# Three-layer fp32 block: the last feed-forward norm by products with ones, and two weight sums per layer by transfers that add

## The chip, the cores and the metric

One NeuronCore of one Trainium2 chip runs the whole program. The metric is device time in microseconds (us), median of several runs. The engines are TensorE (PE, with its weight loads as PEld), VectorE (DVE), ScalarE (ACT), GpSimd (POOL) and SyncE (SP). [...]

## The reference, cut to what matters

Two blocks follow each other over 512 tokens of width 1024, in fp32: three attention layers in all, and behind each of them a gated feed-forward layer (FFN) with a hidden width of 2816. All else (gated linear attention, band, memory, differential and forgetting attention) stays as it is in the change.

```
x = x + conv_ffn(rmsnorm(x, norm_ffn_g[l]), ...)          # layers 0 and 1
h2 = rmsnorm_2(x, norm2_g[l])                             # layer 2, eps 1e-5
g = jnp.einsum('bsd,df->bsf', h2, w_gate[l])
u = jnp.einsum('bsd,df->bsf', h2, w_up[l])
x = x + jnp.einsum('bsf,fd->bsd', jax.nn.silu(g) * u, w_down[l])
```

In layers 0 and 1 g also goes through a causal convolution of three taps before the silu.

## The kernel before, in words

**Layout.** Activations lie transposed: 1024 features as 8 tiles `X[:, k, :]` of 128 partitions by 512 tokens. Each fp32 operand is split into a high and a low fp32r part (`hH`, `hL` for activations, `WH`, `WL` for weights), and every product is done three times: high by high, low by high, high by low. SP loads weights into six places of `raw`; ACT copies a piece into `WH` (rounding it) and DVE subtracts to get `WL` (steps `conv` for whole units of 128x2048, `cconv` for pieces of 128x1024, "chunks").

**Norms.** The scale of a token, 1/sqrt(mean square), isn't applied to the input but to the products, through `Rsb` (128x512, one row per token repeated over partitions). The squares are added over the 8 tiles into `acc`: tiles 1 to 6 on POOL (`res_norm`, L3264), tile 7 on DVE (`res_last`, L3005). Then there are two ways to sum over the partitions:

- the norms in `ROW_NORMS` ("ffn0", "kv", "ffn1"): ACT and DVE split `acc` into `accH` and `accL` (`row_split`), PE multiplies both by a matrix of ones (two products of 128x512, `row_sums`), so the sums come out on all partitions; ACT takes the root into `Rsb`, DVE inverts all 128x512 of it (`row_inverse`, L2742);
- the norm "n2" of layer 2: PE multiplies four pieces of `acc` by a column of ones (`rstd_first`, L1379), ACT takes the root of 128x4, DVE inverts 128x4, PE spreads that over the partitions with four products by the identity (`rstd_second`, L1391), and ACT copies the result into `Rsb`. These products are in plain fp32.

**The FFN.** The first one or two of 11 steps (`WHOLE` = 2, 2, 1 for layers 0, 1, 2) are done plainly: units of gate and up weights, `whole` or `half` tiles (L1497, L1516). All later steps split the products into blocks A11, A12, A21, A22 by features and gate or up and do seven products in place of eight (`PRODUCTS` = 1, 5, 6, 3, 7, 2, 4; L1846, 24 matmuls of 128x256 each), with sums of inputs (`wtB`, `wtS`, `wtL` make them in `Tf`, `TH`, `TL`) and sums of weights: product 5 needs A21+A22, product 6 adds A11 to that, 3 adds A12 to that of 6, and 7 needs A11+A21. A sum of weights is one DVE addition of 128x1024 (`wsum`, L2547) into `Wsum[0]` (5, 3) or `Wsum[1]` (6, 7), then split by `cconv` like any piece. Products 1, 6, 7 and 4 gather in one PSUM bank and ACT copies it out between them (`wcopy`, L2063): 6 waits for the copy of 1, 3 waits for that of 5, 7 for that of 6, 4 for that of 7.

**Order.** A planner, `order()`, writes one list of steps; each engine walks through it and does its part of each step, in that order, with semaphores between the engines. In the attention output (`out_rest`) eight tiles m = 0..7 come out of PE; for each, DVE adds to `X`, ACT makes `hH` and the square, DVE `hL`, and POOL adds the square to `acc`. In `ffn_wino` the order around the first products is written out by hand; in layer 2 `sum_ahead` puts the first two `wsum` steps between the `wtS` and `wtL` steps, in layers 0 and 1 `conv_ahead` puts them in front of the `cconv` steps. POOL issues the transfers that add the FFN's partial outputs to `X` (`wx`, L3288), DMA with an accumulating write.

Of the kernel before, what the change touches and what calls it, by code (L numbers as in the profile page):

```python
# [34 lines left out]
WHOLE = (2, 2, 1)  # L35
# [8 lines left out]
BLOCKS = {1: ("A11",), 5: ("A21", "A22"), 6: ("A11",), 3: ("A12",), 7: ("A11", "A21"), 2: ("A12",), 4: ("A22",)}  # L44
SUMS = (5, 6, 3, 7)


# [118 lines left out]
def chunk_list():  # L166

    chunks, items, seen = [], [], set()
    for n, u in enumerate(UNITS):
        role = u[6] if len(u) > 6 else None  # L170
        if role is None or role[1] == "T":
            items.append(("unit", n))
            continue
        i = role[0]
        if i in seen:
            continue
        seen.add(i)
        for key in dict.fromkeys(SEQUENCE[i]):
            c = {"key": (i,) + key, "i": i, "sum": None, "unit": None}
            if key[0] == "q":  # L180
                _, s, q = key
                parts = [ROLE[i, b, s] for b in BLOCKS[q]]
                if q in SUMS:
                    c["sum"] = {6: [(i, "q", s, 5)], 3: [(i, "q", s, 6)]}.get(q, []) + parts
                    c["place"] = {5: 0, 6: 1, 3: 0, 7: 1}[q]
                else:
                    c["unit"] = parts[0]
            else:
                c["unit"] = ROLE[(i, "D") + key[1:]]
            items.append(("chunk", len(chunks)))  # L190
            chunks.append(c)
    return chunks, items
# [26 lines left out]
def raw_read_last():  # L219

    out = {}
    for at, (kind, x) in enumerate(ITEMS):
        if kind == "unit":
            out[x] = at, ("wl", x, last_part(x))
            continue
        c = CHUNKS[x]
        for n, when, key in ([(c["unit"], at, ("wl", "c", x))] if c["unit"] is not None else
                             [(y, at - 1.5, ("wg", "sum", x)) for y in c["sum"] if not isinstance(y, tuple)]):
            out[n] = max(out.get(n, (-1, None)), (when, key), key=lambda v: v[0])
    return out  # L230
# [90 lines left out]
def pieces(hd):  # L321
# [3 lines left out]
    if hd % 2 == 0:  # L325
# [11 lines left out]
             "C": ([4, 5, 0, 1, 2, 3, 6, 7], 6)}  # L337
ROW_NORMS = ("ffn0", "kv", "ffn1")
NEXT_NORM = {"A": "ffn0", "B": "ffn1", "C": "n2"}
# [8 lines left out]
def order():  # L348
# [8 lines left out]
    def conv_ahead(end):  # L357
        while now["conv"] < len(ITEMS):
# [204 lines left out]
    def out_rest(stage, nrm):  # L563
# [3 lines left out]
        while opened:  # L567
# [6 lines left out]
            if m:  # L574
                for x in (0, 1) if m == 1 else (m,):
                    tile_done("res_norm", stage, x, nrm)
            m += 1
        for u in range(2, 4):
            n = take()
            for c in (0, 128):  # L580
# [4 lines left out]
                for x in T_SUMS.get(m, ()):  # L585
                    put(x[0], WINO_OF[nrm], x[1])
                m += 1

    def ffn_wino(i, end):
# [16 lines left out]

        def sum_ahead(i):
            c = now["summed"]
            while CHUNKS[c]["i"] < i or not CHUNKS[c]["sum"]:
                c += 1  # L610
            put("wsum", c)
            now["summed"] = c + 1

        def whole(name, m, n):
# [402 lines left out]
def program(nc, wall, xt, memt, colsd, biasd, consts, rope, gatew, out):  # L1017
    ctx = ExitStack()
    with ctx:
# [168 lines left out]
        s_raw = [sem(f"raw{i}") for i in range(6)]  # L1188
        s_part = [sem(f"part{i}") for i in range(2)]
        s_mem = [sem(f"mem{i}") for i in range(4)]  # L1190
        s_x = [sem(f"x{i}") for i in range(8)]
# [113 lines left out]
        def chunk_slot(c):  # L1305
            x = W_AT["chunk", c]
            o = (x % 2) * CHUNK
            return [v[x // 2][:, o:o + CHUNK] for v in (WH, WL)]

        def chunk_src(c):  # L1310
# [648 lines left out]
        def scalar(e):  # L1959
            w, mark = Lane(e), partial(ev.mark, "act")  # L1960

            for what, *a in STEPS:
                if what == "start":
                    src = memt.rearrange("p (k t) -> p k t", k=8)
                    for i in range(4):
                        e.dma_start(mrA[:, 2 * i:2 * i + 2, :], src[:, 2 * i:2 * i + 2, :]).then_inc(s_mem[i], 16)
                    w.wait_ge(*at("eps", 1))
                    e.activation(small[:, 62:63], small[:, 60:61], ACT.Copy).then_inc(*mark("wh", "warm"))
# [20 lines left out]
                elif what == "cconv":  # L1989
                    c = a[0]  # L1990
                    if CHUNKS[c]["sum"]:
                        w.wait_ge(*at("wg", "sum", c))
                    else:
# [137 lines left out]
                elif what == "rstd_first":  # L2131
                    w.wait_ge(*at("sums", a[0]))
                    w.wait_ge(*at("eps", 1))
                    eps = a[1]
# [335 lines left out]
        def vector(e):  # L2470
# [44 lines left out]
            for what, *a in STEPS:  # L2515
# [18 lines left out]
                elif what == "wsum":  # L2534
                    c = CHUNKS[a[0]]
                    src = []
                    for y in c["sum"]:
                        if isinstance(y, tuple):
                            w.wait_ge(*at("wg", "sum", CHUNK_AT[y]))
                            src.append(Wsum[CHUNKS[CHUNK_AT[y]]["place"]][:, :])  # L2540
# [648 lines left out]
        def gpsimd(e):  # L3189
            w, mark = Lane(e), partial(ev.mark, "pool")  # L3190

            for what, *a in STEPS:
                if what == "start":
                    e.memset(diag[:, :], 0.0).then_inc(*mark("set", "zero"))
                    e.memset(gw[:, :, :], 0.0).then_inc(*mark("set", "gw0"))
                    e.memset(small[:, 60:61], 1e-6).then_inc(*mark("eps", 0))
                    e.memset(small[:, 63:64], 1e-11).then_inc(*mark("eps", 2))
                    e.memset(small[:, 61:62], 1e-5).then_inc(*mark("eps", 1))
                    for n, (c, size) in enumerate(V_ONES):
                        e.memset(vA[:, :, c:c + size], 1.0).then_inc(*(mark("set", "vones") if n else mark("set", "vonesh")))  # L3200
                    w.wait_ge(s_K if ev.sems else None, 16)
                    for i, j in ((0, 0), (1, 2), (2, 3)):
                        e.tensor_copy(KB[:, i, :], K[:, j, :]).then_inc(*mark("KB", i))

# [124 lines left out]
        def sync(e):  # L3329
# [34 lines left out]
            for h, k, n in STORES:  # L3364
# [19 lines left out]
        RCOL_USED = {"mix0": [], "kv": [("vev", "vA", 2, 2)], "n1": [("vev", "vB", 2, 2)],  # L3384
                     "n2": [("vev", "fv", 2, 1)], "last": [("spread", "n2")]}

# [129 lines left out]
```

## Time and profile before

| | |
|---|---|
| median of 3 runs | 1771.16 us (1771.16 to 1771.86) |
| profiled execution: its own time, its span | 1771.75 us, 1770.0 us |
| busy, share of the span: PE, PEld, DVE, ACT, POOL | 99%, 86%, 73%, 54%, 12% |
| mean granted TensorE clock | 0.998 of full speed |
| weights and other bytes moved by DMA | 205.19 MB, 116 GB/s on the mean |
| FFN of layer 0, 1, 2 begins (first L1497 product) | 260.54, 827.76, 1413.86 us |

The span runs from the first to the last instruction; the run's own time is 1.75 us longer. A timeline row gives the start, the duration (of all of a merged row's instructions together), engine, line, operation, operands, count, and in brackets the engine's idle time before it with what ended that. PE's rows overlap, since its matmuls are pipelined: what a product costs PE is the distance from its start to the next start, not its duration.

### The profile page before, as it was taken

How to read it: one execution, taken by the hardware profiler on the slowest of the kernel's cores; microseconds unless marked ns; L12 is line 12 of the kernel's file. 1: busy time of each engine (PE TensorE's matmuls, PEld its weight loads, DVE VectorE, ACT ScalarE, POOL GpSimd, SP SyncE). 2: the span in 40 equal slices, each digit the busy share in tenths (PEclk: the TensorE clock that was granted, in tenths of full speed). 3: DMA queues.
4: the chain of work that ended last, by engine and by line, in shares of the span. 5: the costliest groups of instructions: out<-in, count | busy, mean ns of one | idle time of the engine just before them, and what ended most of it. 6: DMA issues, size and time to landing. Idle time of an engine off the chain costs nothing.

```text
span 1770.0 us, 26240 instructions
## 1 busy us (share of the span) xinstructions
PE 1759.2 (99%) x10680; PEld 1527.0 (86%) x10680; DVE 1295.2 (73%) x1794; ACT 950.3 (54%) x1442; POOL 203.7 (12%) x223
## 2 busy tenths in 40 slices
PE   9999999999999999999999999999999999999998
PEld 7877788999999887787899999977777899999997
DVE  6878568888786765646888787689767487776765
ACT  6645444655555544755465555552567455454454
POOL 0001220110111200002011110103001101111110
PEclk9999999999999999999999999999999999999999
DMA  6221223654545342212364554443221236555442
GB/s 250 72 90 66 71 95 108 155 138 137 143 127 136 89 158 99 96 49 93 98 178 113 154 127 140 111 119 107 73 96 50 103 99 151 135 143 143 109 141 73
DMA packets 61623, 205.19 MB, mean 116 GB/s; under 512 B 7344, under 2 KB 9520, under 8 KB 53184
## 3 DMA queue, kind: packets, MB, share of 16 engines
q1 hardware_dynamic: 38832, 162.55, 27.6%
q0 software_dynamic: 17280, 31.46, 10.0%
q10 hardware_dynamic: 5392, 9.51, 1.7%
q8 instruction: 85, 1.39, 0.3%
q14 instruction: 34, 0.28, 0.0%
HBM read 169.38 MB, written 2.13 MB: 97 GB/s over the span
## 4 chain that ended last, share of the span: by engine, by line
PE 89%; DVE 6%; ACT 3%; issue 1%; DMA 1%; ACTq 0%; DVEq 0%; POOL 0%; SPq 0%
PE ps L1846 31%; PE ps L1497 17%; PE ps L1872 16%; PE ps L1411 6%; PE ps L1536 4%; PE ps L1659 2%; PE ps L1704 2%; PE ps L1556 2%; PE ps L1684 2%; PE ps L1895 2%; DVE WL L2531 1%; PE ps L1743 1%; PE ps L1724 1%; PE ps L1913 1%; ACT WH L1986 1%
## 5 line engine op out<-in xcount | busy, mean ns | idle before, releaser
L1846 PE MATMUL ps<-hH,WH 128*128 128x256 f32 x896 | 253.9, 283 | 0.8 <-ACT held L2063 0.8
L1846 PE MATMUL ps<-hH,WL 128*128 128x256 f32 x896 | 254.0, 283 | 0.0
L1846 PE MATMUL ps<-hL,WH 128*128 128x256 f32 x896 | 253.9, 283 | 0.0
L2553 DVE TENSOR_TENSOR WL<-raw,WH 128x1024 fp32r<-128x1024 f32 x138 | 168.2, 1220 | 113.1 <-ACT WH L1997 113.1
L2531 DVE TENSOR_TENSOR WL<-raw,WH 128x1024 fp32r<-128x1024 f32 (+1 forms) x137 | 167.5, 1260 | 89.3 <-ACT WH L1986 88.9
L1497 PE MATMUL ps<-hH,WH 128*128 128x512 f32 x528 | 208.7, 395 | 0.3 <-DVE WL L2531 0.3
L1497 PE MATMUL ps<-hH,WL 128*128 128x512 f32 x528 | 205.9, 390 | 0.0
L1497 PE MATMUL ps<-hL,WH 128*128 128x512 f32 x528 | 205.9, 390 | 0.0
L3288 POOL DMA_DIRECT2D X<-sq x120 | 104.8, 959 | 866.3 <-ACT sq L2052 864.4
L1846 PE MATMUL ps<-TH,WL 128*128 128x256 f32 x672 | 190.5, 283 | 0.0
L1846 PE MATMUL ps<-TL,WH 128*128 128x256 f32 x672 | 190.4, 283 | 0.0
L1846 PE MATMUL ps<-TH,WH 128*128 128x256 f32 x672 | 190.4, 283 | 0.0
L2553 DVE TENSOR_TENSOR WL<-Wsum,WH 128x1024 fp32r<-128x1024 f32 x112 | 136.7, 1221 | 68.4 <-ACT WH L1997 68.2
L1986 ACT ACTIVATE WH<-raw 128x1024 fp32r<-128x1024 f32 (+1 forms) x137 | 134.5, 1028 | 78.8 <-PE ps L1497 39.6
L1846 PEld LDWEIGHTS ps<-hH,WH 128*128 128x128 f32 x896 | 172.1, 192 | 2.1 <-ACT held L2063 1.0
L1846 PEld LDWEIGHTS ps<-hL,WH 128*128 128x128 f32 x896 | 172.2, 192 | 1.2
L1846 PEld LDWEIGHTS ps<-hH,WL 128*128 128x128 f32 x896 | 172.1, 192 | 0.0
L1872 PE MATMUL ps<-FH,WH 128*128 128x512 f32 x432 | 168.9, 391 | 0.0
L1872 PE MATMUL ps<-FL,WH 128*128 128x512 f32 x432 | 168.9, 391 | 0.0
L1872 PE MATMUL ps<-FH,WL 128*128 128x512 f32 x432 | 168.3, 389 | 0.0
L1997 ACT ACTIVATE WH<-raw 128x1024 fp32r<-128x1024 f32 x138 | 144.5, 1053 | 19.5 <-PE ps L1846 16.8
L1997 ACT ACTIVATE WH<-Wsum 128x1024 fp32r<-128x1024 f32 x112 | 118.0, 1054 | 55.6 <-PE ps L1846 42.4
(442 smaller groups left out, 3897.7 us busy)
## 6 DMA issues: line engine op xcount, KB each, us to landing
raw<-in_wall SPq DMA_DIRECT2D x166, 512.0 KB, 4.3
raw<-in_wall SPq DMA_DIRECT2D x65, 1024.0 KB, 4.8
X<-sq POOLq DMA_DIRECT2D x120, 256.0 KB, 4.0
bias<-in_bias ACTq DMA_DIRECT2D x12, 256.0 KB, 3.0
raw<-in_wall SPq DMA_DIRECT2D x8, 256.0 KB, 7.0
X<-in_xt SPq DMA_DIRECT2D x8, 256.0 KB, 7.8
CB<-rows ACTq DMA_DIRECT2D x8, 256.0 KB, 3.4
out_y<-X SPq DMA_DIRECT2D x8, 256.0 KB, 2.2
```

The lines of the kernel that those rows point to most:

```text
L1411: mm = e.matmul(ps[b][:, :], ww[:, k, c:c + 128], x, start=(k == seq[0] and i == 0), stop=(k == seq[-1] and i == 2))
L1497: mm = e.matmul(ps[b][:, 0:N], ww[:, k, c:c + 128], x[:, k, 0:N], start=(k == 0 and i == 0), stop=(k == 7 and i == 2))
L1536: mm = e.matmul(o, x[:, k, t * 128:t * 128 + 128], ww[:, k, :], start=(k == 0 and i == 0), stop=(k == 7 and i == 2))
L1556: mm = e.matmul(ps[b][:, :], x[:, k, t * 128:t * 128 + 128], ww[:, kx, :], start=(k == 0 and i == 0), stop=(k == 7 and i == 2))
L1659: mm = e.matmul(ps[b][:, c:c + L], queries[u["kind"]][r, u["m"], t * 128:t * 128 + 128], keys[u["kind"]][r, u["m"], 0:L], start=opens, sto ...
L1846: mm = e.matmul(ps[b][:, 256 * u:256 * u + 256], ww[:, p, 128 * u:128 * u + 128], x, start=(opens and p == 0 and u == 0 and n == 0), stop= ...
L1872: mm = e.matmul(ps[BANK["wd", i, g, m]][:, :], ww[:, kx, mi * 128:mi * 128 + 128], x[:, f % 8, :], start=(kx == 0 and n == 0), stop=(kx == ...
L1986: e.activation(WH[W_AT["unit", n] // 2][:, c], unit_raw(n)[:, c], ACT.Copy).then_inc(*mark("wh", n, x))
L1997: e.activation(chunk_slot(c)[0], chunk_src(c), ACT.Copy).then_inc(*mark("wh", "c", c))
L2531: e.tensor_tensor(WL[v][:, c], unit_raw(n)[:, c], WH[v][:, c].bitcast(F32), ALU.subtract).then_inc(*mark("wl", n, x))
L2553: e.tensor_tensor(L, chunk_src(c), H.bitcast(F32), ALU.subtract).then_inc(*mark("wl", "c", c))
L3288: e.dma_start(X[:, m, :], part[m % 2][:, :], accum_op=ALU.add).then_inc(s_part[m % 2], 16)
```

## The change

The norm "n2" joins `ROW_NORMS`, so that layer 2 goes the way of layers 0 and 1 (its epsilon stays in column 61), and the other branch of `ffn_wino` goes. For the first seven-product step of each layer the sums for products 5 and 6 are no longer made by DVE: POOL issues, among the last steps of the attention output, two plain transfers of 512 KB from the weights in memory into `Wsum[0]` and `Wsum[1]` (behind tile m = 1), one accumulating transfer into each (behind m = 3) and a third into `Wsum[1]` (behind m = 5), five for each layer. A transfer that adds waits on POOL until the one before it into the same place has landed. The blocks themselves are still loaded into `raw` for the other products. `sum_ahead` goes; ACT's `cconv` of these two pieces and DVE's sum for product 3 wait for the transfers' semaphores. Two groups of POOL's semaphore marks become part of another one, with the same waits.

```
+DMA_SUMS = {5: ("A21", "A22"), 6: ("A11", "A21", "A22")}
+DMA_ROUNDS = (((0, 5, 0), (1, 6, 0)), ((0, 5, 1), (1, 6, 1)), ((1, 6, 2),))
+DMA_AT = {1: 0, 3: 1, 5: 2}
...
+                c["dma"] = s == WHOLE[i] and q in DMA_SUMS
...
-ROW_NORMS = ("ffn0", "kv", "ffn1")
+ROW_NORMS = ("ffn0", "kv", "ffn1", "n2")
...
-                        if CHUNKS[c]["sum"]:
+                        if CHUNKS[c]["sum"] and not CHUNKS[c]["dma"]:
                             put("wsum", c)
...
+            if m in DMA_AT:
+                put("wdma", WINO_OF[nrm], DMA_AT[m])
...
-        if st in ROW_NORMS:
-            put("row_split", st)
+        put("row_split", st)
         n = take()
-        if st in ROW_NORMS:
-            put("sqrt_table", st)
+        put("sqrt_table", st)
         whole("g", 0, n)
-        if st in ROW_NORMS:
-            put("wtS", i, 1)
-            half(1, n, 0)
-            put("row_sums", st, 60)
-            put("wtL", i, 1)
-            half(1, n, 1)
-            put("row_inverse", st)
-            put("wtB", i, 2)
-            put("wtS", i, 2)
-        else:
-            put("rstd_first", st, 61)
-            put("wtS", i, 1)
-            put("wtL", i, 1)
-            put("wtB", i, 2)
-            put("wtS", i, 2)
-            whole("g", 1, n)
-            put("rstd_second", st)
+        put("wtS", i, 1)
+        half(1, n, 0)
+        put("row_sums", st, 61 if i == 2 else 60)
+        put("wtL", i, 1)
+        half(1, n, 1)
+        put("row_inverse", st)
+        put("wtB", i, 2)
+        put("wtS", i, 2)
         done.add(n)
-        if WHOLE[i] == 1:
-            sum_ahead(i)
         put("wtL", i, 2)
         put("wtB", i, 3)
         if WHOLE[i] == 1:
             put("wtS", i, 3)
-            sum_ahead(i)
             put("wtL", i, 3)
...
                 elif what == "cconv":
                     c = a[0]
                     if CHUNKS[c]["sum"]:
-                        w.wait_ge(*at("wg", "sum", c))
+                        w.wait_ge(*summed(c))
...
+                elif what == "wdma":
+                    i, r = a
+                    w.wait_ge(*at("out", OUT_OF[i], 0))
+                    for x, pn, n in DMA_ROUNDS[r]:
+                        if n:
+                            w.wait_ge(s_wsum[x] if ev.sems else None, 16 * (len(DMA_SUMS[pn]) * i + n))
+                        y = ROLE[i, DMA_SUMS[pn][n], WHOLE[i]]
+                        src = wall[:, WOFF[y]:WOFF[y + 1]]
+                        if n:
+                            e.dma_start(Wsum[x][:, :], src, accum_op=ALU.add).then_inc(s_wsum[x], 16)
+                        else:
+                            e.dma_start(Wsum[x][:, :], src).then_inc(s_wsum[x], 16)
```

## Rows read from the trace of the kernel before

**Rows 1.** The page: busy time, share of the span and instructions of each engine.

```profile
PE 1759.2 (99%) x10680; PEld 1527.0 (86%) x10680; DVE 1295.2 (73%) x1794; ACT 950.3 (54%) x1442; POOL 203.7 (12%) x223
```

**Rows 2.** PE's waits in the whole span: total, times, longest, in us.

```profile
PE ps L1421 <- POOL diag L3194: 1.4, 1, 1.4
...
PE ps L1846 <- ACT held L2063: 0.8, 1, 0.8
```

**Rows 3.** Timeline of PE in layer 2, start of the FFN to the third of the seven products.

```profile
1413.86 0.39 PE L1497 MATMUL ps<-hH,WH 128*128 128x512 f32 x1
...
1426.50 0.48 PE L1497 MATMUL ps<-hH,WH 128*128 128x512 f32 x1
...
1437.47 0.28 PE L1846 MATMUL ps<-hH,WH 128*128 128x256 f32 x1
...
1443.23 0.28 PE L1846 MATMUL ps<-TH,WH 128*128 128x256 f32 x1
```

**Rows 4.** Timeline of PE in layer 0, first gate tile and first up tile.

```profile
260.54 0.39 PE L1497 MATMUL ps<-hH,WH 128*128 128x512 f32 x1
...
271.88 0.39 PE L1497 MATMUL ps<-hH,WH 128*128 128x512 f32 x1
```

**Rows 5.** Timeline of PE in layer 1, products 1, 5 and 3 of the first seven-product step.

```profile
879.92 0.28 PE L1846 MATMUL ps<-hH,WL 128*128 128x256 f32 x1
880.18 0.35 PE L1846 MATMUL ps<-TH,WH 128*128 128x256 f32 x1
...
886.91 0.39 PE L1846 MATMUL ps<-hH,WH 128*128 128x256 f32 x1 [0.77 <-ACT held L2063]
```

**Rows 6.** Timeline of DVE in layer 0, from the last square to the third low part.

```profile
263.36 0.67 DVE L3005 TENSOR_TENSOR acc<-acc,sq 128x512 f32<-128x512 f32 x1
...
271.54 3.35 DVE L2742 RECIPROCAL Rsb<-Rsb 128x512 f32<-128x512 f32 x1
...
277.42 0.96 DVE L2583 TENSOR_TENSOR TL<-Tf,TH 128x768 fp32r<-128x768 f32 x1 [0.92 <-ACT TH L2010]
```

**Rows 7.** Timeline of DVE in layer 2, from the last square to the sum for product 3.

```profile
1417.56 0.68 DVE L3005 TENSOR_TENSOR acc<-acc,sq 128x512 f32<-128x512 f32 x1
...
1426.08 1.22 DVE L2547 TENSOR_TENSOR Wsum<-raw,raw 128x1024 f32<-128x1024 f32 x1
1427.21 0.95 DVE L2583 TENSOR_TENSOR TL<-Tf,TH 128x768 fp32r<-128x768 f32 x1
...
1431.92 1.21 DVE L2553 TENSOR_TENSOR WL<-raw,WH 128x1024 fp32r<-128x1024 f32 x1
...
1435.39 1.21 DVE L2547 TENSOR_TENSOR Wsum<-Wsum,raw 128x1024 f32<-128x1024 f32 x1
```

**Rows 8.** Timeline of ACT in layer 2, from the last high part to the copy of product 1.

```profile
1430.03 0.85 ACT L2010 ACTIVATE TH<-Tf 128x768 fp32r<-128x768 f32 x1 [2.11 <-DVE Tf L2576]
...
1437.76 2.01 ACT L1997 ACTIVATE WH<-Wsum 128x1024 fp32r<-128x1024 f32 x2 [4.97 <-PE ps L1497]
...
1442.13 0.58 ACT L2063 ACTIVATE held<-ps 128x512 f32<-128x512 f32 x1
```

**Rows 9.** Timelines of DVE and ACT in layer 1: second sum, copy of product 5.

```profile
877.68 1.22 DVE L2547 TENSOR_TENSOR Wsum<-Wsum,raw 128x1024 f32<-128x1024 f32 x1
...
886.28 0.58 ACT L2063 ACTIVATE held<-ps 128x512 f32<-128x512 f32 x1
```

**Rows 10.** Timeline of POOL in layer 2: adds of squares 3 and 4, and of square 6.

```profile
1403.20 3.25 POOL L3264 TENSOR_TENSOR acc<-acc,sq 128x512 f32<-128x512 f32 x2 [4.17 <-ACT sq L2338]
...
1415.37 1.72 POOL L3264 TENSOR_TENSOR acc<-acc,sq 128x512 f32<-128x512 f32 x1 [4.33 <-ACT sq L2338]
```

**Rows 11.** Accumulating transfers by source line (ns, landing in us), and issues of weight loads.

```profile
L3288 POOL DMA_DIRECT2D X<-sq x120: 850/862/1236, 311.8 to 1739.2; - x120
...
DMA to landing us min/median/max: 3.2/4.0/9.1
...
raw<-in_wall SPq DMA_DIRECT2D x166, 512.0 KB, 4.3
```

More of the change, by code:

```diff
@@ L178, in chunk_list @@
         for key in dict.fromkeys(SEQUENCE[i]):
-            c = {"key": (i,) + key, "i": i, "sum": None, "unit": None}
+            c = {"key": (i,) + key, "i": i, "sum": None, "unit": None, "dma": False}
             if key[0] == "q":
@@ L227, in raw_read_last @@
         for n, when, key in ([(c["unit"], at, ("wl", "c", x))] if c["unit"] is not None else
-                             [(y, at - 1.5, ("wg", "sum", x)) for y in c["sum"] if not isinstance(y, tuple)]):
+                             [(y, at - 1.5, ("wg", "sum", x)) for y in c["sum"]
+                              if not c["dma"] and not isinstance(y, tuple)]):
             out[n] = max(out.get(n, (-1, None)), (when, key), key=lambda v: v[0])
@@ L586, in out_rest @@
                     put(x[0], WINO_OF[nrm], x[1])
+                if m in DMA_AT:
+                    put("wdma", WINO_OF[nrm], DMA_AT[m])
                 m += 1
@@ L605, in ffn_wino @@
         st = FFN_NORMS[i]
[L607 to L612, printed above, removed]
         def whole(name, m, n):
@@ L1189, in program @@
         s_part = [sem(f"part{i}") for i in range(2)]
+        s_wsum = [sem(f"wsum{i}") for i in range(2)]
         s_mem = [sem(f"mem{i}") for i in range(4)]
@@ L1308, in chunk_slot, with summed @@
             return [v[x // 2][:, o:o + CHUNK] for v in (WH, WL)]
+        def summed(c):
+            c = CHUNKS[c]
+            if c["dma"]:
+                x = c["place"]
+                return (s_wsum[x] if ev.sems else None), 16 * len(DMA_SUMS[c["key"][3]]) * (c["i"] + 1)
+            return at("wg", "sum", CHUNK_AT[c["key"]])
         def chunk_src(c):
@@ L1966, in scalar @@
                         e.dma_start(mrA[:, 2 * i:2 * i + 2, :], src[:, 2 * i:2 * i + 2, :]).then_inc(s_mem[i], 16)
-                    w.wait_ge(*at("eps", 1))
+                    w.wait_ge(*at("set", "eps1"))
                     e.activation(small[:, 62:63], small[:, 60:61], ACT.Copy).then_inc(*mark("wh", "warm"))
@@ L2132, in scalar @@
                     w.wait_ge(*at("sums", a[0]))
-                    w.wait_ge(*at("eps", 1))
+                    w.wait_ge(*at("set", "eps1"))
                     eps = a[1]
@@ L2538, in vector @@
                         if isinstance(y, tuple):
-                            w.wait_ge(*at("wg", "sum", CHUNK_AT[y]))
+                            w.wait_ge(*summed(CHUNK_AT[y]))
                             src.append(Wsum[CHUNKS[CHUNK_AT[y]]["place"]][:, :])
@@ L3195, in gpsimd @@
                     e.memset(gw[:, :, :], 0.0).then_inc(*mark("set", "gw0"))
-                    e.memset(small[:, 60:61], 1e-6).then_inc(*mark("eps", 0))
-                    e.memset(small[:, 63:64], 1e-11).then_inc(*mark("eps", 2))
-                    e.memset(small[:, 61:62], 1e-5).then_inc(*mark("eps", 1))
+                    e.memset(small[:, 60:61], 1e-6).then_inc(*mark("set", "eps0"))
+                    e.memset(small[:, 63:64], 1e-11).then_inc(*mark("set", "eps2"))
+                    e.memset(small[:, 61:62], 1e-5).then_inc(*mark("set", "eps1"))
                     for n, (c, size) in enumerate(V_ONES):
@@ L3202, in gpsimd @@
                     for i, j in ((0, 0), (1, 2), (2, 3)):
-                        e.tensor_copy(KB[:, i, :], K[:, j, :]).then_inc(*mark("KB", i))
+                        e.tensor_copy(KB[:, i, :], K[:, j, :]).then_inc(*mark("set", "KB", i))
                 elif what == "fence":
@@ L3384, in program @@
         RCOL_USED = {"mix0": [], "kv": [("vev", "vA", 2, 2)], "n1": [("vev", "vB", 2, 2)],
-                     "n2": [("vev", "fv", 2, 1)], "last": [("spread", "n2")]}
+                     "last": [("vev", "fv", 2, 1)]}
         SQ_USED = {("ffn0", 1): [("cvD", "k", 5, 3)], ("ffn0", 2): [("cvD", "k", 4, 3)],
```

## The prediction, made before the change was run

> **What bounds the kernel now.** I read the page first: PE is busy 99% of the span, DVE 73% [rows 1]. That share overstates PE, so I looked at the distance between starts, which is what a product costs. In layer 2 the 48 products of 128x512 from 1426.50 to 1437.47 take 0.229 us each, the 48 of 128x256 from there to 1443.23 take 0.12 us each [rows 3]: PE goes at one pace without a hole. Then I read the view of waits, for PE alone: nine entries in the whole span, from 1.4 us at the start to 0.2 us, and only one of them in the part that the change touches, 0.8 us before a seven-product step (L1846) [rows 2]. So work taken from DVE is worth time only where PE waits for it, and work that is added to DVE or POOL costs time only where it makes PE wait. Two numbers decide: what PE itself no longer does, and which product is late next.
>
> **PE's own work, layer 2.** From the first gate product to the first up product layer 2 takes 1426.50 - 1413.86 = 12.64 us [rows 3], layer 0, which already goes the new way, 271.88 - 260.54 = 11.34 us [rows 4], for the same 48 products. The next 48 take 10.97 us [rows 3], 0.09 over the 10.88 of 48 starts at layer 0's pace (11.34 us less two sum products, 50 products in all: 0.227 each). PE is thus done with its plain products 1.30 + 0.09 = 1.39 us earlier. Product 1 could start at 1437.47 - 1.39 = 1436.08 and product 6 at 1443.23 - 1.39 = 1441.84, if their weights and copies are there.
>
> **What DVE and ACT gain and lose in layer 2.** Added: ACT's high and DVE's low part of `acc`, a full 128x512 inversion of 3.35 us (in layer 0's row [rows 6]). Removed: two sums of 1.22 us [rows 7]. These sums stood where DVE would otherwise wait for ACT: in layer 0, without them, the low part at 277.42 had 0.92 us of waiting ahead of it [rows 6], in layer 2 the one at 1427.21 had none behind the sum at 1426.08 [rows 7]. So much of the removed work was free. I follow the new chain with intervals between rows:
>
> - DVE's last square of layer 2 stays at 1417.56 [rows 7].
> - In layer 0 the inversion begins 271.54 - 263.36 = 8.18 us behind that square, and the low part of the third input sum 277.42 - 271.54 = 5.88 us behind the inversion [rows 6]. In layer 2 that gives 1425.74 and 1431.62; the latter stood at 1427.21 before, so it is 4.4 us later.
> - From there to ACT's high part of the last input sum: 1430.03 - 1427.21 = 2.82 us [rows 7, 8], so 1434.44.
> - From that to DVE's low part of product 1's weights: 1431.92 - 1430.03 = 1.89 us [rows 7, 8], so 1436.33, done 1.21 us later at 1437.54. Product 1 can't start at 1436.08; it starts at about 1437.65, 0.2 us later than before. PE's whole gain is eaten here.
> - From product 1's low part to the sum for product 3 (two low parts and two scalings of gate tiles lie between): 1435.39 - 1431.92 = 3.47 us [rows 7], so 1439.80 to 1441.01.
> - ACT walks its list in order. It copies product 3's weights only behind that sum, and behind that copy stand a table load, two silus and the copy of product 1 out of PSUM. Before, the sum was long done and ACT waited for PE (4.97 us); the pair of weight copies ended at 1437.76 + 2.01 = 1439.77, and product 1's copy began 2.36 us later, at 1442.13 [rows 8]. Now: 1441.04 + 1.00 (half the pair) + 2.36 = 1444.40, done 0.58 us later at 1444.98.
> - Product 6 goes on in the bank of product 1, so it waits for that copy: about 1445.03 against 1443.23 [rows 3]. **Layer 2: +1.8 us.**
>
> Behind it product 3 needs product 5's copy, about three ACT operations later; ACT is now 2.27 us behind its old place and PE 1.8 us, so 0.5 us of whatever slack was there goes. I add nothing for it. The bounds of this term are -1.39 us (the chain is shorter than I think and nothing binds) and +2.8 us (another half to one microsecond lost on the chain).
>
> **Layer 1.** PE starts product 5 at 880.18, 0.26 us behind the last start of product 1, instead of 0.12; product 3 starts at 886.91, 6.73 us later instead of 48 x 0.12 = 5.76 us, and waits there 0.77 us for ACT [rows 5]: for the copy of product 5, which began at 886.28 [rows 9]. Together 0.14 + 0.97 = 1.1 us. ACT is late there behind DVE, and two sums of 1.22 us go from DVE's list in front of it (the second stood at 877.68 [rows 9]). 2.4 us is more than the wait, so I take the whole of it: **-1.1 us**; the bounds are -1.1 and 0. **Layer 0** has no such wait [rows 2], and the same sums go there for nothing: 0, with 0 on both sides as far as DVE is concerned.
>
> **The transfers.** Nothing of them is on PE. What they add is on POOL's list, which works in order: five issues a layer, and waits for landings ahead of the adds of squares. An issue of 256 KB that adds costs POOL 0.86 us (up to 1.24), its landing takes 3.2 to 9.1 us, 4.0 in the median; a plain load of 512 KB lands in 4.3 us [rows 11]. No row shows an adding transfer of 512 KB out of memory. Bounds: 4.0 us, as if the size cost nothing, and 18 us, twice the longest row; for the issue 0.86 and twice that. I take 6 us and 0.86 us, since the double size of a load costs little over the adding row's median. In layer 2 the third square is added from 1403.20 to about 1404.8 [rows 10]. The plain loads, issued some 6 us before, have landed (4.3 us). The two first adding transfers go out at 1404.8 and 1405.7, the last must wait for the second of them: 1411.7 with 6 us. The add of square 6 begins at 1415.37 [rows 10]; to issue in front of it, the landing may take until 1415.37 - 0.86 = 1414.5, so 8.8 us. That idle time of POOL (4.33 us before that add) is what hides the last wait; if it is gone, the add of square 6, DVE's last square and everything above moves. Price taken: 0. The sums themselves are used first at about 1436, some 20 us after the last issue, and in layers 0 and 1 later still, so no weights are late. 15 transfers of 512 KB are 7.9 MB on top of 205 MB; I see nothing that waits for weight loads.
>
> Of a transfer that GpSimd issues the Trainium skill says (SBUF — State Buffer, "SBUF: two separate sides" and "A bandwidth-pool intuition that's wrong (but worth ruling out)") that its descriptors can't be written while VectorE holds the shared port in a two-port operation, and gives 3100 ns for one of 620 ns. This trace shows no such thing: 120 issues beside a busy VectorE, none over 1.24 us [rows 11]. With five issues of 3.1 us the add of square 6 would end some 3 us later, and that would be the second rival below by another way.
>
> **Sum.** +1.8 - 1.1 + 0 + 0 = +0.7 us on the profiled execution, 1771.75 to 1772.45 us. That execution lies 0.6 us above the median, so I forecast **1771.9 us** as the median: no change that can be told, since about 0.2% (3.5 us) is what a measurement of this kernel tells from no change.
>
> **Rivals.**
>
> - *Nothing binds in layer 2.* The intervals from layer 0 don't carry over, DVE's list has room, and PE keeps its 1.39 us, with layer 1's 1.1: -2.5 us, 1768.7 us. For it: DVE is 73% busy. Against: every interval is of the same instructions in the same order, and product 1's weights had only 1437.47 - 1433.1 = 4.3 us of slack (1431.92 + 1.21), against 4.4 us of delay and PE's 1.39 us. Chance 0.2.
> - *Slower: POOL stands in front of the add of square 6.* The second adding transfer lands later than 8.8 us behind its issue. The place is the last wait of POOL, between the adds of squares 5 and 6. Each microsecond over that moves DVE's last square (after some 0.5 us: 1417.56 against 1415.37 + 1.72 = 1417.09 [rows 7, 10]), and with it product 6 of layer 2 one for one. At 12 us: 3.2 - 0.5 = 2.7 us in layer 2, and between 0 and 2.7 us in each of layers 0 and 1, whose first sums stand behind the same add: 0.7 + 2.7 to 8.1, so 1774.6 to 1780.0; I price it at 1776. It decides for slower from about 12 us. For it: one row in the trace has 9.1 us at half the size, and weight loads run at the same time. Against: the median of 4.0 us. Chance 0.14.
> - *The sums weren't what ACT waited for in layer 1.* Its wait stays, layer 2 loses its 1.8: 1773.0 us. Against it: two sums ahead of it in the same list. Chance 0.1.
>
> **How the numbers follow.** The forecast has 0.56. The range reaches from the first rival (1768.7, a little under for the spread of runs) to where the slower one begins: 1768.3 to 1775.5 us; left out is most of the slower rival and little else, under 0.2. Faster by over 0.2% (under 1767.6) would take more than all that PE waits and does less for together, 2.5 us: 0.03. Slower by over 0.2% (above 1774.7): most of the slower rival, 0.13. Within: 0.84.
>
> **What would show it.** In the profile after: no L1379 and L1391 row near 1420 and 1426, two products of `accH` and `accL` in their place, and u's first product about 11.35 us behind g's; product 1 of layer 2 waiting for DVE's WL, product 6 for ACT's copy (a wait of 1 to 2 us <- held); PE's wait in layer 1 gone. POOL's idle time before the add of square 6 still there. Wrong would make it: PE without waits in layer 2 (then 1768.7), or adds of square 6 released by a DMA.

## The result, and the profile after

The changed kernel takes **1777.8 us** (median of 6, 1777.32 to 1779.62), the one before 1771.35 us (median of 6) beside it: ratio 1.0037, 95% interval 1.0024 to 1.005. It is slower by 6.4 us. The forecast was 1771.9 us, its range 1768.3 to 1775.5 us, so it was wrong.

The profiled execution of after has 1777.8 us and a span of 1776.1 us, 6.1 us more than before. Busy shares hardly move (compare [rows 1]):

```profile
PE 1759.0 (99%) x10666; PEld 1523.9 (86%) x10666; DVE 1300.2 (73%) x1789; ACT 950.8 (54%) x1443; POOL 214.6 (12%) x238
```

PE is busy for 0.2 us less than before, so the 6 us are waits. The waits of PE, as in [rows 2] (total, times, longest, in us; line numbers of after stand three lower than those of before, L1494 is L1497; `issue` means that the profile shows nothing that PE waited for):

```profile
PE ps L1843 <- DVE WL L2550: 2.2, 1, 2.2
PE ps L1494 <- issue: 1.8, 2, 0.9
PE ps L1843 <- ACT held L2060: 1.4, 1, 1.4
...
PE ps L1494 <- DVE hL L2478: 1.1, 3, 0.4
...
PE ps L1383 <- DVE accL L2485: 0.7, 1, 0.7
```

The first and third are the two that the prediction expected in layer 2. The others stand at the start of the feed-forward parts, where it expected nothing. The timeline of PE, layer 1 (first gate tile, second half tile, sums by ones, product 3), then layer 2 (last product ahead of the first gate tile, first gate tile, half tile, first up tile, products 1 and 6):

```profile
829.38 0.47 PE L1494 MATMUL ps<-hH,WH 128*128 128x512 f32 x1 [0.87 <-issue]
...
834.78 0.47 PE L1494 MATMUL ps<-hH,WH 128*128 128x512 f32 x1 [0.38 <-DVE hL L2478]
...
839.12 0.47 PE L1383 MATMUL ps<-accH,ones_r 128*128 128x512 f32 x1 [0.66 <-DVE accL L2485]
...
889.29 0.28 PE L1843 MATMUL ps<-hH,WH 128*128 128x256 f32 x1
...
1415.75 0.39 PE L1408 MATMUL ps<-fqr,WL 128*128 128x512 f32 x1
...
1417.06 0.47 PE L1494 MATMUL ps<-hH,WH 128*128 128x512 f32 x1 [0.93 <-issue]
...
1422.46 0.47 PE L1494 MATMUL ps<-hH,WH 128*128 128x512 f32 x1 [0.36 <-DVE hL L2478]
...
1429.13 0.39 PE L1494 MATMUL ps<-hH,WH 128*128 128x512 f32 x1
...
1442.32 0.35 PE L1843 MATMUL ps<-hH,WH 128*128 128x256 f32 x1 [2.15 <-DVE WL L2550]
...
1449.73 0.39 PE L1843 MATMUL ps<-TH,WH 128*128 128x256 f32 x1 [1.44 <-ACT held L2060]
```

A product of 128x512 follows the one before it by 0.23 us; the first gate tile of layer 2 follows by 1417.06 - 1415.75 = 1.31 us, so 1.08 us are lost there, and the layer as a whole came 2.12 us late (1415.75 + 0.23 against 1413.86 [rows 3]). Pairing the same products of both traces all along the span gives where the 6.1 us arise:

| place | how late PE is once past it | what the place adds |
|---|---|---|
| ahead of layer 0's feed-forward part | -0.60 us | -0.60 |
| start of layer 0 | +0.15 | +0.75 |
| the attention part behind it | +0.6 | +0.45 |
| start of layer 1, to its first up tile | +3.47 | **+2.9** |
| layer 1's first seven-product step | +2.28 | **-1.2** |
| up to layer 2 | +2.12 | -0.16 |
| start of layer 2, to the half tile | +3.93 | **+1.8** |
| layer 2 up to its first up tile (the norm) | +2.54 | **-1.4** |
| layer 2, product 1 | +4.93 | **+2.4** |
| layer 2, product 6 | +6.61 | **+1.7** |
| end | +6.1 | -0.5 |

The -0.60 us ahead of layer 0 belongs to the profiled execution of before, whose span is 0.7 us or more above the median of that kernel: each of the thirteen other kernels is 0.4 to 0.7 us earlier there. The 0.75 us at the start of layer 0 stand only in the kernels that issue where the change does (after, and 2 and 4 below); all others have 0.0 there. The 0.45 us behind it are scatter between executions, of 0 to 1.7 us, at 609 to 618 us: kernels 5 and 10 below, which differ in layer 2 alone, have 0.0 and 1.7 us.

Where the late starts come from is seen on POOL and DVE ahead of layer 2 (start, duration of the row, in brackets the idle time before it). POOL, the answer to [rows 10]:

```profile
1398.24 1.47 POOL L3261 TENSOR_TENSOR acc<-acc,sq 128x512 f32<-128x512 f32 x1 [29.94 <-ACT sq L2335]
1399.66 1.17 POOL L3298 DMA_DIRECT2D Wsum<-in_wall  x2
1400.81 1.34 POOL L3261 TENSOR_TENSOR acc<-acc,sq 128x512 f32<-128x512 f32 x1
1406.34 1.72 POOL L3261 TENSOR_TENSOR acc<-acc,sq 128x512 f32<-128x512 f32 x1 [4.19 <-ACT sq L2335]
1408.00 1.82 POOL L3296 DMA_DIRECT2D Wsum<-in_wall  x2
1409.18 1.94 POOL L3261 TENSOR_TENSOR acc<-acc,sq 128x512 f32<-128x512 f32 x1
...
1418.30 0.87 POOL L3296 DMA_DIRECT2D Wsum<-in_wall  x1 [2.57 <-DMA Wsum<-in_wall]
1420.06 1.70 POOL L3261 TENSOR_TENSOR acc<-acc,sq 128x512 f32<-128x512 f32 x1 [0.90 <-ACT sq L2335]
```

and DVE in the same stretch:

```profile
1400.28 4.09 DVE L2528 TENSOR_TENSOR WL<-raw,WH 128x1024 fp32r<-128x1024 f32 x2 [1.73 <-ACT WH L1983]
...
1408.35 3.07 DVE L2565 SCALAR_TENSOR_TENSOR T7f<-X,cols,Tf 128x256 f32<-128x256 f32 x1
...
1415.73 2.36 DVE L2528 TENSOR_TENSOR WL<-raw,WH 128x1024 fp32r<-128x1024 f32 x2 [1.27 <-ACT WH L1983]
...
1422.24 0.68 DVE L3002 TENSOR_TENSOR acc<-acc,sq 128x512 f32<-128x512 f32 x1
```

The adds of squares 1 and 2 and those of 3 and 4 used to follow each other without a gap (3.25 us for the second pair [rows 10]). Now two issues stand between the adds of each pair. DVE's instruction of 128x256 takes 0.48 us when nothing disturbs it; here it begins at 1408.35 and ends at 1411.42, 0.3 us behind the end of the add of square 4 (1409.18 + 1.94 = 1411.12). It is held through both issues and the add. The pair of weight parts ends at 1404.37, 2.2 us behind the end of the add of square 2 (1402.15), about its whole undisturbed length (2.36 us). DVE was held before the change too, but only to the earlier end of the adds:

```profile
1398.16 3.08 DVE L2531 TENSOR_TENSOR WL<-raw,WH 128x1024 fp32r<-128x1024 f32 x2 [1.73 <-ACT WH L1986]
...
1405.22 1.51 DVE L2568 SCALAR_TENSOR_TENSOR T7f<-X,cols,Tf 128x256 f32<-128x256 f32 x1
```

The issues so cost DVE 1.0 + 1.55 = 2.55 us, and its last square comes 1422.24 - 1417.56 [rows 7] = 4.68 us late, the layer's 2.12 and these 2.56. The first gate tile starts (1417.06) 0.1 us behind the end of the first of the two weight parts at 1415.73 (half of 2.36 us further on, about 1416.9); so what the profile calls `issue` fits a wait for DVE.

The wait that the second rival was about is not the cause: POOL does wait 2.57 us for a landing, but is done 0.90 us before ACT releases the add of square 6. The issues cost about 0.6 us (plain) and 0.9 us (adding) each, near the 0.86 us taken. The nine transfers that add land in 5.4 to 9.4 us, 7.6 in the median, not in the 6 us taken; the one that POOL waits for here took 9.4 us, over the 8.8 us that the prediction allowed, and was hidden because the add of square 6 was late too (1420.06 against 1415.37 [rows 10]). What it would cost with that add in its old place no run shows.

### The profile page after: what moved, and what is told of

It is laid out like the page before. It is cut to its first block, busy times and chain, and to the rows that moved or that the text cites. A ratio compares the mean times of both kernels' runs of the same rounds, so it can differ in the third digit from the quotient of the medians.

```text
span 1776.1 us, 26223 instructions
## 1 busy us (share of the span) xinstructions
PE 1759.0 (99%) x10666; PEld 1523.9 (86%) x10666; DVE 1300.2 (73%) x1789; ACT 950.8 (54%) x1443; POOL 214.6 (12%) x238
## 3 DMA queue, kind: packets, MB, share of 16 engines
q8 instruction: 85, 1.39, 0.3%
HBM read 177.25 MB, written 2.13 MB: 101 GB/s over the span
## 4 chain that ended last, share of the span: by engine, by line
PE 87%; DVE 7%; ACT 4%; issue 1%; DMA 1%; ACTq 0%; DVEq 0%; POOL 0%; SPq 0%
PE ps L1843 31%; PE ps L1494 17%; PE ps L1869 16%; PE ps L1533 4%; PE ps L1408 3%; DVE WL L2528 2%; PE ps L1656 2%; PE ps L1701 2%; PE ps L1553 2%; PE ps L1681 2%; PE ps L1892 2%; PE ps L1740 1%; ACT hH L2327 1%; ACT WH L1983 1%; PE ps L1721 1%
## 5 line engine op out<-in xcount | busy, mean ns | idle before, releaser
L1494 PE MATMUL ps<-hH,WH 128*128 128x512 f32 x520 | 206.0, 396 | 3.1 <-issue 1.8
L1494 PE MATMUL ps<-hL,WH 128*128 128x512 f32 x520 | 202.9, 390 | 0.0
L1494 PE MATMUL ps<-hH,WL 128*128 128x512 f32 x520 | 202.8, 390 | 0.0
```

The costliest lines, as they stand in the source:

```text
L1494: mm = e.matmul(ps[b][:, 0:N], ww[:, k, c:c + 128], x[:, k, 0:N], start=(k == 0 and i == 0), stop=(k == 7 and i == 2))
```

## Experiments

All times are medians in us, "before" beside them on the same chip; "span" is the median over a kernel's executions of the difference to the span of before.

| | kernel | time | before | ratio (95%) | span |
|---|---|---|---|---|---|
| 1 | issues moved off the adds | 1775.27 | 1771.05 | 1.0020 (1.0012 to 1.0029) | +3.3 |
| 2 | adding transfers of 8 columns | 1777.69 | 1771.05 | 1.0037 (1.0024 to 1.0051) | +5.9 |
| 3 | norm alone | 1774.18 | 1771.05 | 1.0016 (1.0007 to 1.0025) | +2.0 |
| 4 | transfers alone | 1774.60 | 1771.05 | 1.0019 (1.0010 to 1.0028) | +3.6 |
| 5 | 1, gate weights ahead of the last transfer | 1772.13 | 1770.68 | 1.0007 (0.9998 to 1.0016) | +0.6 |
| 6 | repeat of 5 | 1772.25 | 1770.68 | 1.0009 (1.0000 to 1.0018) | +1.0 |
| 7 | transfers alone, as in 5 | 1769.55 | 1770.68 | 0.9994 (0.9985 to 1.0002) | -1.1 |
| 8 | 5, silus behind the copy of product 1 | 1771.85 | 1770.75 | 1.0007 (0.9997 to 1.0016) | +0.2 |
| 9 | 8, weights of products 1, 5 earlier | 1771.10 | 1770.75 | 1.0001 (0.9992 to 1.0010) | -0.2 |
| 10 | 5 and 14 small products | 1771.43 | 1770.75 | 1.0004 (0.9995 to 1.0013) | +0.6 |
| 11 | 7, plain loads between the adds | 1770.76 | 1770.73 | 1.0000 (0.9991 to 1.0009) | 0.0 |
| 12 | 7, first adding transfers between the adds | 1770.96 | 1770.73 | 1.0001 (0.9993 to 1.0010) | +0.2 |

**1. The issues moved.**

```diff
-DMA_AT = {1: 0, 3: 1, 5: 2}
+DMA_AT = {2: 0, 4: 1, 7: 2}
```

> The whole change, with the same five issues per layer, but none between two adds of squares that follow each other on POOL: the plain loads behind the add of square 2, the first two adding transfers behind the add of square 4, the last behind the add of square 6. Theory (place on POOL's list): an issue ahead of an add makes the add end later, and DVE's next instruction with two SBUF inputs waits for that add; with the issues moved, the adds stand where they stood before, the first gate product of layers 1 and 2 starts without a stall, layer 1 keeps its gain of 1.1 us, and layer 2 loses the 1.8 us of the prediction's chain: +0.7 us, about 1772 us. Rival A (traffic): the 7.9 MB of extra transfers delay the other loads wherever they are issued: 1777 us or more. Rival B (the issue itself blocks DVE wherever it stands): DVE's weight parts beside the moved issues take about 1.2 and 1.8 us longer, and the time is 1776 us or so.

POOL and DVE ahead of layer 2 in this kernel:

```profile
1397.57 2.90 POOL L3261 TENSOR_TENSOR acc<-acc,sq 128x512 f32<-128x512 f32 x2 [29.94 <-ACT sq L2335]
1400.40 1.17 POOL L3298 DMA_DIRECT2D Wsum<-in_wall  x2
1404.65 3.25 POOL L3261 TENSOR_TENSOR acc<-acc,sq 128x512 f32<-128x512 f32 x2 [3.07 <-ACT sq L2335]
1407.84 1.80 POOL L3296 DMA_DIRECT2D Wsum<-in_wall  x2
```
```profile
1399.61 3.08 DVE L2528 TENSOR_TENSOR WL<-raw,WH 128x1024 fp32r<-128x1024 f32 x2 [1.73 <-ACT WH L1983]
...
1406.66 1.52 DVE L2565 SCALAR_TENSOR_TENSOR T7f<-X,cols,Tf 128x256 f32<-128x256 f32 x1
1408.10 0.47 DVE L2569 SCALAR_TENSOR_TENSOR Tf<-X,small,Tf 128x256 f32<-128x256 f32 x1
```

The holds are back at 3.08 and 1.52 us, and the stalls of the gate tiles of layers 1 and 2 are gone. Rival B falls: beside the adding issues (1407.84 to 1409.64) DVE's next instruction with two inputs in SBUF runs in 0.47 us. Layer 2 behaves as predicted: seen from its first gate tile, which is 1.44 us late, PE gains 1.4 us up to the up tile, product 1 is late by 0.24 us, product 6 by 1.93. Yet the time misses the 1772 us by 3.3 us, and one wait of PE is new. DVE, then PE, in layer 1:

```profile
837.44 0.23 DVE L2777 TENSOR_TENSOR gw<-graw,gg 128x64 f32<-128x64 f32 x1 [5.25 <-DMA graw<-in_gatew]
837.58 0.68 DVE L2485 TENSOR_TENSOR accL<-acc,accH 128x512 fp32r<-128x512 f32 x1
```
```profile
838.41 0.47 PE L1383 MATMUL ps<-accH,ones_r 128*128 128x512 f32 x1 [2.45 <-DVE accL L2485]
```

DVE waits 5.25 us for 32 KB of gate weights; before it waited 1.64. ACT issued that load 1.3 us behind POOL's last adding transfer, and the low part of the squares stands behind it on DVE's list. So rival A holds in this one place.

**2. Issues without their traffic.**

```diff
-e.dma_start(Wsum[x][:, :], src, accum_op=ALU.add)
+e.dma_start(Wsum[x][:, 0:8], src[:, 0:8], accum_op=ALU.add)
```

> The whole change, its issues where it put them, but each adding transfer carries 8 of 1024 columns (so the sums are only their first term outside these). Theory (place on POOL's list): the issues cost POOL the same, so the adds of squares 2 and 4 stay late, the stalls at the start of layers 1 and 2 stay, and the time is 1777 to 1778 us; only the last POOL wait and the later landing of the gate weights (1.1 us of DVE's waiting in layer 1, some 0.8 us of PE's) may go. Rival A (traffic): with three of five transfers gone the stalls go, 1772 to 1774 us.

1777.69 us, where the change has 1777.8: the stalls of the gate tiles are all there (1.8 us up to the half tile in each of layers 1 and 2, as in the change), though three of five transfers carry almost nothing; PE's wait for the low part of the squares in layer 1 is gone (PE loses 0.0 us there, 0.9 in the change), and DVE waits 1.71 us for the gate weights, not 2.76. So these stalls come from the issues' place on POOL's list, not from their bytes; the 0.9 us go with the bytes.

**3 and 4. Each part of the change alone.** The norm alone keeps `sum_ahead` and both sums on DVE:

```diff
-DMA_SUMS = {5: ("A21", "A22"), 6: ("A11", "A21", "A22")}
+DMA_SUMS = {}
...
-DMA_AT = {1: 0, 3: 1, 5: 2}
+DMA_AT = {}
...
```

The transfers alone keep the two-step norm of layer 2:

```diff
-ROW_NORMS = ("ffn0", "kv", "ffn1", "n2")
+ROW_NORMS = ("ffn0", "kv", "ffn1")
...
```

> The norm of the last feed-forward part by products with ones, both first weight sums by DVE as before: no transfer into the sums. Theory: the starts of the layers are untouched; layer 1 keeps its wait of 0.8 us (no gain of 1.1); layer 2 has the chain of the prediction, with two sums of 1.22 us in it that hide partly in waits of 0.91 us for ACT: product 6 late by 1.8 to 3 us, so 1773 to 1774.5 us. Rival (the norm is the costly part of the change): 1776 us or more.

> The sums by adding transfers, issued where the change issues them, with the last norm as before. Theory (place on POOL's list): the stalls at the start of the layers stay, 0.5 us in layer 0, 3.0 in layer 1, 1.7 in layer 2, layer 1 gains 1.1 us: +4.1 us, about 1775.5 us. Rival (the norm is the costly part): about 1770 us.

The norm alone costs 3.1 us, 2.0 of them in the span. From the first gate tile of layer 2 PE gains 1.4 us, then product 1 is 0.44 us late and product 6 2.13 us: the prediction's chain, with 0.2 us for the two sums that still stand in it. The transfers alone cost 3.6 us: start of layer 0 +0.75, start of layer 1 +2.9, its first step -1.2, start of layer 2 +1.8, as in the whole change. So both parts cost; neither alone explains the 6.4 us.

**5 and 6. The gate weights first.** Kernel 5 is kernel 1 ("the kernel before this one" of its expectation) with one wait more:

```diff
 w.wait_ge(*at("out", OUT_OF[i], 0))
+if (i, r) == (1, 2):
+    w.wait_ge(s_gw if ev.sems else None, 48)
```

> The whole change with its issues moved as in the kernel before this one, and in layer 1 the last adding transfer is issued only when the gate weights (32 KB) have landed. Theory (the small load was slow because a 512 KB transfer was issued 1.3 us before it): DVE waits 1.6 us for the gate weights as it did before the change, PE's wait of 2.4 us for the low part of the squares in layer 1 goes, layer 1 gains its 1.1 us, layer 2 loses 1.8 us as the prediction has it. Span +0.7 us on that of before, time 1772 to 1773 us. Rival (the gate weights come late for the first two adding transfers, or the loads of weights): the wait of 2.4 us stays, 1775 us.

> As the kernel before it, and in layer 2 the table load and the two silus of ACT stand behind the copy of product 1 out of PSUM, not ahead of it. Theory (product 6 waits for that copy, which stands 2.4 us further down ACT's list than it need): product 1 is still late by 0.2 us, product 6 starts 0.12 us x 48 = 5.76 us behind it without a wait, so layer 2 loses 0.2 us in place of 1.8 and layer 1 keeps its 1.1 us: span 0.9 us below that of before, time 1770 to 1771.5 us. Rival: the silus are late for product 7 or 3 then, and the 1.6 us come back there: as the kernel before it.

Kernel 5 has the span that the prediction gave for the whole change: +0.6 us in the median over 11 executions, forecast +0.7. In the profiled execution PE loses 0.4 us at the sums by ones in place of 2.7 (DVE still waits 2.90 us for the gate weights there, 1.70 in kernel 7, which issues the same way), layer 1's first step gains 1.2 us, and layer 2 loses 1.92 us (products 1 and 6):

```profile
1436.26 0.36 PE L1843 MATMUL ps<-hH,WH 128*128 128x256 f32 x1 [1.40 <-DVE WL L2550]
...
1443.67 0.39 PE L1843 MATMUL ps<-TH,WH 128*128 128x256 f32 x1 [1.42 <-ACT held L2060]
```

Its time is 1.45 us above before all the same: part of it lies outside the span (below, 10). Kernel 6 moved `wy0`, but the silus are issued by `wt0`: the order of instructions on PE, ACT, DVE and POOL is that of 5, so it says nothing on its theory and shows how well a time repeats: 1772.25 against 1772.13 us.

**7. The transfers alone, out of the way** (5 with the norm of before).

> The transfers alone, issues moved and the gate weights ahead of the last one, with the last norm as before the change. Theory: no stall at the start of a layer, layer 1 gains 1.1 us, layer 2 changes by nothing: span 1.1 us below that of before, 1770 us. Rival (the transfers cost something wherever they are issued): 1771 us or more.

1769.55 against 1770.68 us, 1.1 us faster, span -1.1 us, as expected. PE has no wait at the start of a layer and none in layer 1's first step; layer 2 adds nothing. It is the fastest of all kernels here, and each of its 11 executions (1768.9 to 1770.0 us) is below each of the 27 of before (1770.28 to 1771.8), though the interval just reaches 1.

**8 and 9. The end of layer 2's chain.** 8 puts `wt0` and `wy0` behind the copy of product 1; 9 also takes the weights of products 1 and 5 ahead of the fourth input sum:

```diff
-for m in (0, 1):
-    put("wt0", f"g{i}", m)
-put("wy0", i, 0)
...
-later([("wt7", i)], [("wu0", f"u{i}", 0)], ...
+later([("wt0", f"g{i}", 0), ("wt0", f"g{i}", 1), ("wy0", i, 0), ("wt7", i)], [("wu0", f"u{i}", 0)], ...
```
```diff
+if WHOLE[i] == 1:
+    n = take()
+    conv_ahead(len(UNITS))
 put("wtB", i, 3)
...
```

> As the kernel whose last adding transfer waits for the gate weights, and on ACT's list of layer 2 the copy of product 1 out of PSUM stands ahead of the table load and the two silus, not behind them (the kernel before it was meant to do that and moved the step that multiplies on DVE, so that no engine's list changed: it was a repeat). Theory: PE's wait of 1.4 us ahead of product 6 goes, that of 1.4 us ahead of product 1 stays; span 1.5 us below that kernel's, so 1768 us, 0.9 us below before; time about 1770.5 us. Rival (ACT is late behind it anyhow): product 7 or 3 waits for what is later now, and the span stays at 1769.5 to 1770.

> As the one before, and in layer 2 the weight copies of products 1 and 5 (ACT's high, DVE's low part) stand ahead of the fourth input sum, not behind it. Theory: product 1 starts without its wait of 1.4 us; product 6 can't start before ACT's copy of product 1 ends, some 0.7 us earlier than in the kernel before: span 0.7 to 1.4 us lower again, 1766.7 to 1767.4 us, time about 1769.5 us. Rival: the fourth input sum is late then for products 5 and 6, and nothing is won.

Each takes away the wait it aims at, and a later one comes in its place. In 8, product 6 starts without a wait, then product 3 waits for the copy of product 5; in 9, products 1 and 6 come earlier (0.6 us of wait left) and product 3 waits longer (PE, product 3 in 8, then in 9):

```profile
1445.39 0.39 PE L1840 MATMUL ps<-hH,WH 128*128 128x256 f32 x1 [0.92 <-ACT held L2057]
```
```profile
1445.51 0.39 PE L1844 MATMUL ps<-hH,WH 128*128 128x256 f32 x1 [1.71 <-ACT held L2061]
```

Behind that, seen from its first gate tile, layer 2 has lost 1.4 us in 8 and 1.3 us in 9, against 1.9 us in 5. The rival of 8 is the nearer: most of the wait comes back, since ACT's list is late as a whole (it waits 2.73 us in 8 and 2.27 us in 9 for DVE ahead of product 3's weights), and the 1.4 us that PE saves on the norm find no use. Kernel 9 gains 0.4 us of the 0.7 to 1.4 expected.

**10. As many products as before.**

```diff
 w.wait_ge(*at("rowL", a[0]))
+if a[0] == "n2":
+    for _ in range(14):
+        e.matmul(ps[b][:, 0:64], ones_r[:, :], accH[:, 0:64], start=True, stop=True)
 row_sums(b, (accH, accL), ("sums", a[0]))
```

> The kernel whose last adding transfer waits for the gate weights, with 14 small products (128x64, overwritten by the sums that follow) ahead of the sums by ones in layer 2, so that PE has as many products as before the change. They fall into the time by which product 1 waits, so the span stays within 0.5 us. It looks at the time beyond the span, which is 1.70 to 1.86 us in every execution of before and 1.7 to 3.4 us in the kernels with the new norm: if it hangs on the number of PE's instructions, it is 1.7 to 1.9 us in all executions here; if on something else in the norm, it scatters as in the others.

The time beyond the span is 1.72 to 1.83 us in all 11 executions, and 1.71 to 2.93 us in the 11 of kernel 5. The span is the same (+0.6 us), and the time, with more to do, is 0.7 us above before in place of 1.45.

**11 and 12. One pair of issues back between the adds.**

```diff
-DMA_AT = {2: 0, 4: 1, 7: 2}
+DMA_AT = {1: 0, 4: 1, 7: 2}   # 11
+DMA_AT = {2: 0, 3: 1, 7: 2}   # 12
```

> The transfers alone with the last norm as before and all issues moved but one pair: the two plain loads of a layer stand between the adds of squares 1 and 2 again, as in the change. Theory: the hold of DVE there costs DVE 1.0 us in each layer (its pair of weight parts 4.1 us in place of 3.1), and PE nothing, since DVE has some 1.4 us in hand at the start of layers 1 and 2 (it lost 2.5 us with both pairs between adds, and PE's first stall was 1.1 us): time as with all issues moved, 1769.6 us on that chip. Rival (each hold costs PE its own length): 1 us more for each of layers 1 and 2, 1771.5 us.

> The same with the two adding transfers between the adds of squares 3 and 4 as in the change, and the plain loads moved. Theory: DVE is held 3.0 us at its instruction of 128x256 in place of 1.5 in each layer, so it is 1.5 us late, of which 0.1 to 0.3 us reach PE at the start of layers 1 and 2 (1.4 and 1.2 us in hand): time 0.2 to 0.6 us above the kernel with all issues moved, so the 3.0 us and 1.7 us of the change came only from the two holds together. Rival (each hold costs PE its own length): 3 us above it, 1772.6 us.

DVE is held as expected (11: the pair of weight parts 4.1 us; 12: 3.0 us on the instruction of 128x256). Against kernel 7 the spans are 1.1 and 1.3 us longer, more than the theory's 0 and 0.2 to 0.6, less than the rival's 2 and 3; with both pairs between the adds it is 3.6 + 1.1 = 4.7 us (kernel 4, which also has the gate weights late). The time in hand was mis-sized: not the first gate tile but the second half tile waits first. In 12:

```profile
832.55 0.47 PE L1505 MATMUL ps<-hH,WH 128*128 128x512 f32 x1 [0.39 <-DVE hL L2489]
```

In 12 layers 1 and 2 lose 0.8 us each up to there, in 11 0.25 us each, in the change 1.8 us each. DVE's delays of 1.5, 1.0 and 2.55 us less about 0.8 us give 0.7, 0.2 and 1.75. So DVE has 0.8 us in hand, and the two holds add up beyond it. In layer 0 either hold alone costs PE 0.0 us, and both together 0.75. The profiled execution of 11 has another 0.6 us at 609 to 618 us, the scatter named above.

## Why the prediction was wrong

**The step that failed** is "Price taken: 0" for the transfers. It rested on one wait of POOL's, the last, and that wait was indeed hidden, with POOL idle 0.90 us ahead of the add of square 6, though in part by luck: the landing took 9.4 us where 6 were taken and 8.8 allowed, and the add itself was late. The other four issues were counted, 0.86 us each, but not followed: what stands behind them on POOL's list is the add of square 2 and that of square 4, and DVE waits for the end of these adds though no semaphore says so. The trace of before held the hint, the two rows of DVE shown above, 1.51 us for an instruction of 0.48 beside the adds of [rows 10], but only POOL's row was read. Measured: 0.75 us at the start of layer 0 and 1.8 us at that of each of layers 1 and 2 (kernels 1, 2, 11 and 12 show that it is the place of the issues); in layer 2 the whole 2.56 us, since there the chain behind DVE's last square passes them on one for one. Another 0.9 us in layer 1 come from the transfers' bytes, by way of the gate weights (0.0 in kernel 2); the rest up to its first up tile is 0.2. Together the transfers cost 0.75 + 2.9 + 2.56 = 6.2 us in the profiled execution, where the sum had 0.

The Trainium skill has the rule (SBUF — State Buffer, "SBUF: two separate sides" and "Who interferes with whom"): a DVE instruction with two inputs in SBUF contends with a GpSimd instruction that reads SBUF, and whichever starts second waits for the whole of the other. This trace agrees on the hold, with 0.48 us stretched to 1.51 beside two adds and to 3.07 beside two adds with two issues between them; that the first to start wins the rows don't bear out, since DVE's row begins at 1408.35 and that of the add it waits for at 1409.18. The prediction cited the same page for the other direction (issues slowed by DVE), which no run here shows.

**The rivals.** The second rival has the right sign, and its span of outcomes (1774.6 to 1780.0 us) holds the result, but by another mechanism, so that is luck: the landing of over 8.8 us did come in layer 2 (9.4 us), and the add of square 6 didn't wait for it. The first, nothing binds in layer 2, falls: even with the list eased twice (kernel 9) layer 2 loses 1.3 us. The third falls too: layer 1's wait went.

**What held.** PE's own work in layer 2: -1.39 forecast, -1.4 in kernels 1, 3 and 5. The chain: product 1 +0.2 and product 6 +1.8 forecast, +0.24 and +1.93 measured with the issues out of the way. In the change itself, where DVE starts 2.56 us later, each interval still holds. DVE (last square, inversion, low part, product 1's weights, third sum) and ACT (copy of product 1):

```profile
1422.24 0.68 DVE L3002 TENSOR_TENSOR acc<-acc,sq 128x512 f32<-128x512 f32 x1
...
1430.42 3.35 DVE L2739 RECIPROCAL Rsb<-Rsb 128x512 f32<-128x512 f32 x1
...
1436.30 0.96 DVE L2580 TENSOR_TENSOR TL<-Tf,TH 128x768 fp32r<-128x768 f32 x1 [0.91 <-ACT TH L2007]
...
1440.95 1.23 DVE L2550 TENSOR_TENSOR WL<-raw,WH 128x1024 fp32r<-128x1024 f32 x1
...
1444.42 1.22 DVE L2544 TENSOR_TENSOR Wsum<-Wsum,raw 128x1024 f32<-128x1024 f32 x1
```
```profile
1449.10 0.58 ACT L2060 ACTIVATE held<-ps 128x512 f32<-128x512 f32 x1
```

8.18, 5.88, 4.65 (forecast 2.82 + 1.89), 3.47 and 4.68 us (forecast 4.60). Layer 2 lost 6.61 - 2.12 = 4.5 us; 1.8 + 2.56 is 4.4. Layer 1's first step: -1.1 forecast, -1.2 measured, and product 3 at 889.29 no longer waits. So the sum of the other terms, +0.7 us, was right: -1.2 and +1.92 us in kernel 5. That its span is +0.6 us fits this only in part, since it also holds some 0.5 us of the gate weights at the start of layer 1 and scatter elsewhere.

**What was not foreseen besides**: the gate weights (0.66 us of PE's waiting in the change, 2.45 us in kernel 1), and the time beyond the span. Why the time beyond the span grows stays open.

## What to carry to other kernels

When instructions are put into an engine's queue, list what stands behind each of them, not only behind the one that waits, and look for engines that stand still beside that queue without a semaphore: an instruction that takes three times its usual duration in the trace before is such a place. Two delays that are each in part hidden add up past the time in hand (0.25 us a layer for one, 0.8 for the other, 1.8 for both). Work taken from the bound engine pays only if the lists that feed its next product get shorter too: here PE's 1.4 us went to DVE and ACT, and the fastest kernel keeps the old norm.

## What the runs showed of the hardware

- An issue on POOL alone doesn't hold DVE (kernel 1: 0.47 us beside two adding issues), but with an add queued right behind two issues DVE was held from 1408.35, 0.8 us before the row of the add begins (the change). When the add took hold of what DVE waits for isn't shown.
- Of two adding transfers of 512 KB issued 0.6 us apart, the first landed in 5.4 to 7.6 us and the second in 8.0 to 9.4 us (the change, three layers); the plain ones took 3.8 to 4.6 us.
- A small load (32 KB) issued from ACT's queue 1.3 us behind an adding transfer of 512 KB from POOL's took 5.2 us to land (kernel 1), in place of 1.6 before; 5.6 us behind one it took 2.7 us (the change); with the order turned round DVE waited 2.90 us (kernel 5) and 1.70 us (kernel 7) for it, not 5.25.
- The time beyond the span: in 101 executions of before and 55 of five kernels with 10,680 PE instructions it is 1.69 to 1.87 us. In 77 executions of eight kernels with 10,666 it is 1.69 to 3.40 us, over 1.9 us in 46 of them. Fourteen small products put it back to 1.72 to 1.83 us. Why the number or the place of PE's instructions matters isn't shown: the trace has nothing outside the span.
